# Split weights for fp32r matmuls: the low part of a half tile issued in the turn of its high part

## What is computed

```python
def first_block(x, mem, ...):                       # depth 2
    for l in range(DEPTH):
        h = rms_norm(x, norm_g[l])
        z = h @ w_in[l]
        ...                                         # neighbourhood, dilated and memory attention
        y = jnp.concatenate([o_na * silu(na_g), o_dl * silu(dl_g), o_m * silu(m_g)], axis=-1)
        x = x + y @ w_out[l]
    return rms_norm(x, final_g)
```

## Time and profile before

| | |
|---|---|
| median of 3 runs | 3466.97 us (3464.17 to 3470.85) |
| the profiled execution | 3461.89 us, its span 3460.0 us |
| granted TensorE clock, mean | 0.990 |
| share of the chain that ended last, by engine | PE 55%, DVE 6%, ACT 1% |
| transfers | 586.37 MB, mean 169 GB/s; the weights' queue takes 50.3% of 16 engines' span |

### The profile page before, as it was taken

How to read it: one execution, slowest core, us unless ns; L and a number is a source line. 1 busy time by engine, 2 the same in 40 slices (tenths; PEclk the granted TensorE clock), 3 DMA queues, 4 the chain that set the end, 5 groups by cost and what they waited for, 6 DMA issues and landing times.

```text
span 3460.0 us, 68755 instructions
## 1 busy us (share of the span) xinstructions
PE 3367.0 (97%) x30086; PEld 3311.1 (96%) x30086; DVE 2251.8 (65%) x3653; ACT 1616.1 (47%) x2337; POOL 58.6 (2%) x78
## 2 busy tenths in 40 slices
PE   8999999999999899999999999999999999999997
PEld 8999999999998889899999999998999999999997
DVE  6666556557677787696666655687656976666455
ACT  5444444444455434364444444564443644444443
POOL 1000000000000000000000000001000000000000
PEclk9999999999999999999999999999999999999998
DMA  6555555555554223255555556543444465555663
GB/s 237 174 174 178 182 177 174 188 173 176 178 193 149 92 87 100 98 181 196 195 194 194 193 188 194 179 153 105 153 134 134 165 200 195 193 193 191 190 201 125
DMA packets 162493, 586.37 MB, mean 169 GB/s; under 512 B 18128, under 2 KB 18128, under 8 KB 161936
## 3 DMA queue, kind: packets, MB, share of 16 engines
q1 hardware_dynamic: 160560, 574.01, 50.3%
q0 software_dynamic: 1632, 7.96, 0.7%
HBM read 579.80 MB, written 2.10 MB: 168 GB/s over the span
## 4 chain that ended last, share of the span: by engine, by line
PE 55%; DVE 6%; ACT 1%; issue 0%; POOL 0%; ACTq 0%; DVEq 0%; POOLq 0%
PE bank L2133 16%; PE bank L2135 16%; PE bank L2134 16%; DVE pairs L2922 2%; PE bank L2333 1%; PE bank L2346 1%; DVE xs L3038 1%; DVE xs L3036 0%; PE bank L2148 0%; PE bank L2149 0%; PE bank L2150 0%; DVE xr L2926 0%; ACT pairs L2599 0%; ACT xs L2650 0%; DVE right L3386 0%
## 5 line engine op out<-in xcount | busy, mean ns | idle before, releaser
L2133 PE MATMUL bank<-xr,pairs 128*128 128x256 f32 (+1 forms) x5888 | 1661.2, 282 | 34.0 <-DVE pairs L2922 28.1
L2134 PE MATMUL bank<-xr,pairs 128*128 128x256 f32 (+1 forms) x5888 | 1638.2, 278 | 0.0
L2135 PE MATMUL bank<-xr,pairs 128*128 128x256 f32 (+1 forms) x5888 | 1637.8, 278 | 0.0
L2599 ACT ACTIVATE pairs<-raw 128x1024 fp32r<-128x1024 f32 x1106 | 1143.5, 1042 | 965.7 <-PE bank L2135 775.5
L2922 DVE TENSOR_TENSOR pairs<-raw,pairs 128x1024 fp32r<-128x1024 f32 x1106 | 1307.6, 1200 | 357.2 <-ACT pairs L2599 351.1
L2133 PEld LDWEIGHTS bank<-xr,pairs 128*128 128x128 f32 x5888 | 1114.0, 189 | 47.1 <-DVE pairs L2922 30.9
L2134 PEld LDWEIGHTS bank<-xr,pairs 128*128 128x128 f32 x5888 | 1112.7, 189 | 1.4
L2135 PEld LDWEIGHTS bank<-xr,pairs 128*128 128x128 f32 x5888 | 1112.0, 189 | 0.0
L2133 PE MATMUL bank<-parts,pairs 128*128 128x256 f32 x1792 | 496.5, 277 | 0.4 <-DVE parts L2926 0.4
L2134 PE MATMUL bank<-parts,pairs 128*128 128x256 f32 x1792 | 495.0, 276 | 0.0
L2135 PE MATMUL bank<-parts,pairs 128*128 128x256 f32 x1792 | 495.0, 276 | 0.0
(11 more groups left out here) (600 smaller groups left out, 3051.6 us busy)
## 6 DMA issues: line engine op xcount, KB each, us to landing
raw<-in_w_in SPq DMA_DIRECT2D x176, 512.0 KB, 4.7
raw<-in_gate SPq DMA_DIRECT2D x176, 512.0 KB, 5.4
raw<-in_val SPq DMA_DIRECT2D x176, 512.0 KB, 4.3
raw<-in_down SPq DMA_DIRECT2D x160, 512.0 KB, 4.4
raw<-in_l_w_in SPq DMA_DIRECT2D x144, 512.0 KB, 3.9
raw<-in_w_out SPq DMA_DIRECT2D x64, 512.0 KB, 4.6
raw<-in_l_w_out SPq DMA_DIRECT2D x64, 512.0 KB, 3.9
raw<-in_v_in SPq DMA_DIRECT2D x48, 512.0 KB, 5.0
```

The lines of the kernel that those rows point to most:

```text
L2133: mm(o, wh[:, q, :], rh[:, k, :], start=begin and q == 0, stop=False)
L2134: mm(o, wh[:, q, :], rl[:, k, :], start=False, stop=False)
L2135: last = mm(o, wl[:, q, :], rh[:, k, :], start=False, stop=end and q == c - 1)
L2599: e.activation(pair_of(n)[0], v3(raw_of(n), widths[n] // slices[n]), ACT.Copy).then_inc(*hi_made(n))
```

## The change

`load` appends all high parts that are due, and then every low part up to the last of them. The low part of n + 3 is thus appended in the turn of n, where that of n + 2 was.

```diff
         while at_["hi"] < min(n + AHEAD, len(stream)):
             do("hi", at_["hi"])
             at_["hi"] += 1
-            if at_["lo"] < at_["hi"] - 1:
-                do("lo", at_["lo"])
-                at_["lo"] += 1
-        while at_["lo"] <= n:
+        while at_["lo"] < at_["hi"]:
             do("lo", at_["lo"])
             at_["lo"] += 1
         return n
```

## The result

| | before | after |
|---|---|---|
| median | 3466.13 us (3464.17 to 3470.85, 4 runs) | 3558.53 us (3557.24 to 3558.95, 4 runs) |
| profiled execution's span | 3460.0 us | 3556.4 us |
| granted TensorE clock, mean | 0.990 | 0.98 |

The changed kernel takes 1.0263 times as long (95% interval 1.025 to 1.0275): 91 us slower by the ratio, 92 by the medians. The forecast was 3548, the range 3495 to 3605.

What follows compares the result with a forecast made beforehand. TensorE was taken as the bound, busy 3367.0 of 3460.0 us. A with B 66.7, backlogs 8, earlier low parts -3, clock 10: 82 on 3461.9 gives 3544; the median lies 5 higher, so 3548, range 3495 to 3605.

Steps and rivals of the forecast that it cites:

- A: Sums of squares under the second half of l0_w_out and l1_w_out: 7.6 us per half-tile pair, not 5.98; 11.4 us per stretch.
- B: Three stretches making the normalised x: 5.3 us a turn, 2.25 more; 13.7 us each, plus 1.4 where one follows an A.
- The FFN stages and the startup: FFN stages: cost nothing, three turns of slack cover the waits. Startup: nothing to 2 us gained.
- Rival 2: Handovers cost nothing; only the shift by one low part shows, other VectorE waits growing 1.2 us each: 3474; chance 0.10.
- rival 5: Whole kernel: the change does nothing, or all of it hides: 3467; chance 0.02.
- rival 1: The tie is looser than read and the earlier low parts win, ten waits of 17.1 us going: 3450, faster; chance 0.05.
- the clock: Slow TensorE clock after new stalls: two more such stretches for each of the three B, 10 us; bounds 0 and 50.
- the B of mix1: The B that opens the mix1 stage, with no A ahead of it: 13.7 us.
- The tie: VectorE's turn opens with a low part whose high part stands last in ScalarE's list: one handover back and forth per turn.
- Rival 3: The loop costs as said and TensorE stays at 1.2 GHz all through A, 50 in place of 10: 3588; chance 0.07.
- the rest: Outside A and B: 8 us for mixer backlogs, minus 3 for low parts that come earlier; earlier transfers 0.
- Rival 4: The mixers lock too: a third of their turns pays one high part of 1.05 more, 63 us: 3611; chance 0.06.

Runs made afterwards that it cites:

- same3: The changed kernel with both high and low part one turn later (AHEAD 3), so the low part is where the kernel before has it: 3563.67 us, 1.0275.
- ahead5: The kernel before with the high part one turn sooner than in either kernel and the low part where the changed kernel has it, throughout: 3468.87 us, 0.9999.
- mixers_only: The kernel before with the low part early only in half tiles 320 to 419 and 725 to 821 (mixers, first half of w_out): 3489.27 us, 1.0053.
- ab_free: The changed kernel with ScalarE given each high part one turn sooner in the stretches A and B alone: 3483.69 us, 1.0042.
- same5: The changed kernel with both high and low part one turn sooner (AHEAD 5), still in one turn: 3581.65 us, 1.0325.

## Why the prediction was right, and where it was off
**The mechanism was the one forecast.** A: 7.59 us per pair against 7.6 said, and TensorE stands 11.8 and 11.9 us more against 11.4. B: 5.33 us a turn against 5.3. The waits for L2967 and the low part grew where it was said; what had not been named is that a large part of TensorE's waits in B is for L2923 behind the low part. The low part's 43.0 us are less than the 50 and more said. The FFN stages and the startup last as long, within 1 us. Rival 2 (only the shift by one low part costs, 3474) and rival 5 are refuted by same3 and ahead5, rival 1 by the result.

**The stretches, in sum.** For A and B the steps said 66.7 us, and 10 for the clock: 76.7 together. The windows give 73.3, of which 53.6 are standing time and 19.7 longer busy time. In the two B behind an A the standing came to 9.3 and 7.7 us, 15.1 was forecast (13.7 and 1.4). That the sum came so near is in part luck: 13 us too much standing and 10 too little for the clock cancel. As I read it, a TensorE that runs slowly gives VectorE time to catch up, so that part of the wait turns into slow matmuls, and I counted both; no run shows it by itself. In the B of mix1 the loop is interrupted at one place by a longer wait:

```profile
2310.64 1.23 DVE L2919 TENSOR_TENSOR pairs<-raw,pairs 128x1024 fp32r<-128x1024 f32 x1 [4.50 <-ACT pairs L2596]
```

VectorE's low part stands there 4.50 us for a high part. On ScalarE that high part (start 2309.56) is listed behind five small steps of the mixer's own side job, L2810 to L2816, which begin at 2306.85 and include a table load of 1.28 us. The tie lets VectorE wait for them too. The stretch costs 19.0, where 13.7 and some 3 for the clock had been said.

**The clock's term was mis-sized.** I said 10 us, two more stretches at 1.2 GHz in each B. The three B alone took 12.8, near it; but A (6.9) and the mixers (5.2) had been given nothing, and TensorE's busy time rose by 27.1 in all. Rival 3 (1.2 GHz all through A) is refuted: the clock there is 0.97 and 0.95, although TensorE waits seven times for a low part in each A, up to 1.5 us at a time, and once 5.5 us at its end.

**The term that was mis-sized is "the rest": the mixers.** I priced 8 us of backlog, less 3 for waits that go, 5 together; with their share of the clock the windows give 19.8, and mixers_only 18. The step had only counted one low part more ahead of the work that TensorE waits for, the place. What I had missed are more loops like those of A and B. The first is at the opening of the mixer of mix0, where TensorE's wait at L2297 (before L2300) grew from 0.56 to 7.27 us. ScalarE's second L2609 (before L2612) and the L2725 (L2728) that ends this wait, in the changed kernel, in ahead5 and in same3:

```profile
1052.53 0.42 ACT L2609 ACTIVATE arena<-arena 128x256 f32<-128x256 f32 x1 [2.10 <-DVE arena L2927]
...
1071.32 0.42 ACT L2725 ACTIVATE right<-arena 128x256 f32<-128x256 f32 x1 [3.27 <-DVE arena L3202]
```

```profile
1049.13 0.42 ACT L2612 ACTIVATE arena<-arena 128x256 f32<-128x256 f32 x1 [2.10 <-DVE arena L2930]
...
1064.45 0.42 ACT L2728 ACTIVATE right<-arena 128x256 f32<-128x256 f32 x1 [2.31 <-DVE arena L3205]
```

```profile
1057.73 0.42 ACT L2609 ACTIVATE arena<-arena 128x256 f32<-128x256 f32 x1 [2.10 <-DVE arena L2927]
...
1076.53 0.42 ACT L2725 ACTIVATE right<-arena 128x256 f32<-128x256 f32 x1 [3.27 <-DVE arena L3202]
```

From the one to the other it takes 18.79 us in the changed kernel and 18.80 in same3, where the low part is at its old place; it takes 15.32 in ahead5 and 15.31 before (1051.31 to 1066.62). So the tie makes this piece 3.5 us longer, and the place of the low part does nothing to it. The rest of the growth of that wait is that TensorE arrives at it earlier. In the mixer of mix1 the same comparison holds for the wait at L2330 (before L2333), which grew from 2.77 to 8.70 us. From TensorE's L2470 ahead of it to the end of that wait it takes 39.6 us in the changed kernel and in same3, and 34.2 before and in ahead5: 5.4 us for the tie.

Behind L2725 the loop goes on:

```profile
1073.27 1.23 DVE L2919 TENSOR_TENSOR pairs<-raw,pairs 128x1024 fp32r<-128x1024 f32 x1 [1.98 <-ACT pairs L2596]
```

ScalarE's L2725 waits for VectorE's L3202 (3205 before), the high part stands behind L2725, and the low part, tied, stands for it 1.98 us here and 1.49 in the next turn; behind that low part stands the next L3202. The two low parts are 3.37 us apart before and 4.95 after. TensorE's wait has ended by then, so this turn costs it nothing that the profile shows. Rival 4 had this kind of lock, a third of all the mixers' turns for 63 us; here it is met in a few turns. The two pieces make 8.9 us of the mixers' 18 to 20; where the rest comes from stays open. That the tie is behind most of it too is what ahead5 adds to ab_free: loose in the mixers and the rest as well, the kernel is 15 us faster.

By place, then: A and B 3 below the forecast, the mixers 15 above it, places not forecast 3: 96.4 between the spans against 82. That the median is 3558.5 and not 3548 comes for the most part from the mixers.

None of the versions beats the kernel before; ahead5 is level with it, with a low part that is a half tile sooner. That is the answer to what the change was worth without its tie: nothing that can be measured.

## What to carry to other kernels
When two engines with in-order lists feed each other, look how many turns lie between a result and its use in either direction. With nothing between, the turn takes the sum of the pieces that hand over to each other (in B 5.33 us, of 2.6 on VectorE and 2.7 on ScalarE) and not the larger of the two, though neither is busy. Issue the producer a turn ahead of the consumer, rather than both sooner: more lead with the tie (same5) made it worse. Look also at what the producer itself waits for, since a tied consumer inherits it: TensorE's use of an older half tile in same5, a table load in the B of mix1. And read such loops from the distance between two repeats in the timeline, since the total of the waits (643 us in a kernel that loses nothing) doesn't tell.

## What was not expected of the hardware
Arriving earlier at a wait doesn't always pay. In ahead5 TensorE isn't held up for a low part before L2300 in the mixer's opening, arrives there earlier and stands in one piece. TensorE before: the wait for a low part, a window behind it, the wait at L2300, and a window of 31 matmuls from there:

```profile
1062.02 0.40 PE L2133 MATMUL bank<-xr,pairs 128*128 128x256 f32 x1 [1.79 <-DVE pairs L2922]
...
1067.17 0.58 PE L2300 MATMUL bank<-con,right 128*128 128x2 f32 x4 [0.56 <-ACT right L2728]
```

```profile
1062.02:1065.63 3.61, 3.61 (x18) 3.61 (x18) 3.09 (x7) 1.91 (x4) 0.00 (x0) 0.53 0.50 150
1067.20:1070.60 3.40, 3.40 (x31) 3.40 (x31) 3.33 (x8) 2.18 (x6) 0.00 (x0) 1.00 0.52 171
```

And in ahead5:

```profile
1065.01 0.98 PE L2300 MATMUL bank<-con,right 128*128 128x2 f32 x4 [6.80 <-ACT right L2728]
```

```profile
1065.00:1071.40 6.40, 6.39 (x31) 6.40 (x31) 4.66 (x11) 3.03 (x6) 0.00 (x0) 0.50 0.53 168
```

Both kernels lose clock here. Before, the slow stretch (3.61 us at 0.53, nearly all at 1.2 GHz) follows the stand of 1.79 us and lies ahead of L2300, where TensorE has to wait 0.56 us even so: faster matmuls would only have made that wait longer. The matmuls from L2300 on run at 1.00. In ahead5 TensorE stands 6.80 us, is let go 2.2 us sooner, and does the same 31 matmuls at 0.50 (1.2 GHz) in 6.40 us instead of 3.40, with no wait behind them that hides it. What was won by arriving early is lost again. The section "HAM oscillation — how this bites in real kernels" of the Trainium skill's page "TensorE: Matmul & The Clock Gate" says that such a stretch costs half of its length; the trace agrees, 3.0 of 6.40.
